# Retention V as tokens by features, in one doubled chunk, in a one-layer hybrid decoder kernel

## What is computed

```python
h = rmsnorm(x, g_mix)
q_sb, k_sb, v_sb, q_r, k_r, v_r, g_r, gate_sb, gate_ret = split_cols(h @ w_in)
...
q_r = rotary(to_heads(q_r, RET_HEADS))
k_r = rotary(to_heads(k_r, RET_HEADS)) * (RET_QK_DIM ** -0.5)
y_r = retention_chunkwise(q_r, k_r, to_heads(v_r, RET_HEADS))
y_r = from_heads(head_rmsnorm(y_r, ret_norm_gain)) * jax.nn.silu(g_r)
```

## Time and profile before

| what | value |
|---|---|
| median of 3 runs | 907.36 us (907.21 to 907.68) |
| the profiled execution | 907.26 us, its span on the core 905.5 us |
| TensorE busy | 895.5 us, 99% of the span |
| VectorE, ScalarE busy | 515.8 us (57%), 399.7 us (44%) |
| share of TensorE in the chain that ended last | 91% |
| the four pairs | to about 308 us of the span |

### The profile page before, as it was taken

One profiled execution on the slowest core, in us unless ns is written; L12 is line 12 of the kernel. 1 busy time (PEld: TensorE's weight loads), 2 busy tenths in 40 slices (PEclk: granted clock), 3 DMA queues, 4 the chain that ended last, 5 costly groups with the idle time before them and its releaser, 6 DMA issues.

```text
span 905.5 us, 11499 instructions
## 1 busy us (share of the span) xinstructions
PE 895.5 (99%) x4092; PEld 726.9 (80%) x4092; DVE 515.8 (57%) x653; ACT 399.7 (44%) x519; POOL 18.0 (2%) x19
## 2 busy tenths in 40 slices
PE   9999999999999999999999999999999999999998
PEld 7777777777787888888787888888888888888786
DVE  7797677677676443333455556655566543333354
ACT  6656746746746532232345433333333332323431
POOL 1410000000000000000000000000000000000000
PEclk9999999999999999999999999999999999999999
DMA  7114114114114153223322322222222332322131
GB/s 287 70 45 166 48 40 168 46 38 166 52 35 152 48 207 105 83 91 104 117 93 93 116 93 93 93 103 104 94 93 93 90 101 88 105 87 93 61 140 73
DMA packets 28553, 89.93 MB, mean 99 GB/s; under 512 B 3920, under 2 KB 4960, under 8 KB 28400
## 3 DMA queue, kind: packets, MB, share of 16 engines
q1 hardware_dynamic: 27232, 85.87, 27.4%
q10 hardware_dynamic: 1072, 3.67, 1.3%
q0 software_dynamic: 224, 0.06, 0.1%
HBM read 84.34 MB, written 2.10 MB: 95 GB/s over the span
## 4 chain that ended last, share of the span: by engine, by line
PE 91%; DVE 6%; ACT 2%; issue 1%; DMA 1%; SPq 0%; ACTq 0%; DVEq 0%
PE dense L360 28%; PE dense L361 28%; PE dense L362 28%; PE z L417 2%; DVE fs L1102 1%; DVE lo L1105 1%; DVE w_lo L1102 1%; PE aty L448 1%; DMA fs<-in_xT 1%; DVE fs L1286 1%; PE aty L362 1%; PE aty L361 1%; PE aty L360 1%; PE aty L406 1%; ACT w_hi L677 1%
## 5 line engine op out<-in xcount | busy, mean ns | idle before, releaser
L360 PE MATMUL dense<-hi,w_hi 128*128 128x512 f32 x1168 | 462.9, 396 | 1.5 <-DVE lo L1105 0.9
L362 PE MATMUL dense<-hi,w_lo 128*128 128x512 f32 x1168 | 455.2, 390 | 0.0
L361 PE MATMUL dense<-lo,w_hi 128*128 128x512 f32 x1168 | 454.9, 390 | 0.0
L1102 DVE TENSOR_TENSOR w_lo<-w_f,w_hi 128x1024 fp32r<-128x1024 f32 (+2 forms) x160 | 185.6, 1160 | 226.1 <-ACT w_hi L677 225.5
L360 PEld LDWEIGHTS dense<-hi,w_hi 128*128 128x128 f32 x1168 | 219.3, 188 | 52.3 <-issue 4.5
L362 PEld LDWEIGHTS dense<-hi,w_lo 128*128 128x128 f32 x1168 | 219.2, 188 | 46.5
L361 PEld LDWEIGHTS dense<-lo,w_hi 128*128 128x128 f32 x1168 | 219.5, 188 | 43.2 <-issue 1.0
L677 ACT CAST w_hi<-w_f 128x1024 fp32r<-128x1024 f32 (+2 forms) x160 | 158.3, 990 | 181.6 <-PE dense L362 179.0
L662 ACT ACTIVATE fs<-fs 128x512 f32<-128x512 f32 (+2 forms) x79 | 55.4, 707 | 80.7 <-DVE fs L1102 41.5
L1102 DVE TENSOR_TENSOR fs<-fs 128x512 f32<-128x512 f32 (+2 forms) x119 | 87.7, 743 | 3.7 <-ACT fs L709 0.5
L1102 DVE TENSOR_TENSOR lo<-fs,hi 128x512 f32 (+3 forms) x65 | 49.2, 764 | 40.9 <-ACT hi L1037 20.1
(11 more groups left out here) (98 smaller groups left out, 436.6 us busy)
## 6 DMA issues: line engine op xcount, KB each, us to landing
w_f<-in_w_in SPq DMA_DIRECT2D x52, 512.0 KB, 3.3
w_f<-in_w_up SPq DMA_DIRECT2D x44, 512.0 KB, 3.1
w_f<-in_w_down SPq DMA_DIRECT2D x16, 512.0 KB, 3.5
w_f<-in_w_b SPq DMA_DIRECT2D x8, 512.0 KB, 3.2
w_f<-in_w_out SPq DMA_DIRECT2D x8, 512.0 KB, 3.1
w_f<-in_w_pg SPq DMA_DIRECT2D x8, 512.0 KB, 3.1
w_f<-in_w_down SPq DMA_DIRECT2D x8, 384.0 KB, 3.0
fs<-in_xT SPq DMA_DIRECT2D x4, 512.0 KB, 7.0
```

What stands on the lines that cost most here:

```text
L360: mm(out, w1, x1, start=start, stop=False, skip_group_check=skip)
L361: mm(out, w1, x0, start=False, stop=False, skip_group_check=skip)
L362: return mm(out, w0, x1, start=False, stop=stop, skip_group_check=skip)
L1102: return nc.vector.tensor_tensor(out, a, b, op).then_inc(done, 1)
```

## The change

The two V chunks of a pair become one double chunk, `r_v`. The stationary side is now `h` (128 features by 128 tokens, four token blocks) and the moving side is one `k` block of both chunks' weights, 2 x 128 = 256 columns out of two ring slots. The result stands as tokens by features at once, token blocks 0 and 1 in bank 1, 2 and 3 in bank 2. So `turn_v` of chunks 7 and 8 and their copies out of the banks go, and the splits (`high_rv`, `low_rv`) read the two banks directly, at the start of the next `front`; chunk 1 and chunk 2 of that front wait for them (`free_bank`). `r_v` begins once the weights of both chunks are there, and `s_used` rises by 2 at its end. Its 16 steps (one `k` block for half of the tokens each) take the hooks of chunks 7 and 8, of which the head 1 values stand one step later in pairs 1 to 3. `ahead(j, 8)` moves on both engines from the end of `back` to between the two splits in `front`. In the first pair V now uses the normalised `h`, not the raw input, so `low_h(7)` moves forward. Key blocks 2 and 3 of the retention scores become one group: both stand side by side in `z` (384 columns), are masked by one instruction of 512 elements, split together, and their value products stand together at (2, 1). `y_raw` moves in front of `norm_qk(j, 1)` on ScalarE.

```diff
-RAW_OF = {0: 0, 1: 1, 2: 2, 3: 3, 4: 4, 7: 5, 8: 6}
-RAW_X = 8
+RAW_OF = {0: 0, 1: 1, 2: 2, 3: 3, 4: 4}
+RAW_X = 7
+EVACS = 7
...
-        w_hi = [sb(f"w_hi{r}", [P, 8, P], F32R) for r in range(RING)]
+        hi_ring = sb("w_hi", [P, RING, 8, P], F32R)
+        w_hi = [hi_ring[:, r, :, :] for r in range(RING)]
...
+            def r_v(j, hooks, before):
+                c = SLOTS * j + 7
+                pe.wait_ge(s_wlo, c + 2)
+                for step in range(2 * KD):
+                    k, half = step // 2, step % 2
+                    if before and half == 0:
+                        pe.wait_ge(*before[k])
+                    for i in (2 * half, 2 * half + 1):
+                        rows = slice(i * P, (i + 1) * P)
+                        out = bank[1 + half][:, (i % 2) * 2 * P:(i % 2 + 1) * 2 * P]
+                        w1, w0 = hi_ring[:, 1:3, k, :], lo_ring[:, 1:3, k, :]
+                        ins = split3(out, hi[:, T_H + k, rows], lo[:, T_H + k, rows], w1, w0, start=(k == 0 and i % 2 == 0),
+                                     stop=(k == KD - 1), skip=True)
+                    if step == 2 * KD - 1:
+                        ins.then_inc(s_used, 2)
+                    if step in hooks:
+                        hooks[step]()
...
             def free_bank(j, s):
-                pe.wait_ge(s_evac, SLOTS * j + s - 2)
+                if s in (1, 2):
+                    pe.wait_ge(s_raw_done, RAWS * j + s - 2)
+                else:
+                    pe.wait_ge(s_evac, EVACS * j + max(s - 2, 0))
...
-                places = {(0, 1): at(r_scores, prev, 0), (0, 3): at(turn_v, prev, 8, (s_raw_done, RAWS * j - 1)),
-                          (0, 6): at(r_scores, prev, 1), (1, 0): at(r_values, prev, 0), (1, 3): at(r_scores, prev, 2),
-                          (1, 6): at(r_values, prev, 1), (2, 0): at(r_scores, prev, 3), (2, 2): at(r_values, prev, 2),
-                          (2, 5): at(r_values, prev, 3)}
+                places = {(0, 1): at(r_scores, prev, 0), (0, 6): at(r_scores, prev, 1), (1, 0): at(r_values, prev, 0),
+                          (1, 3): at(r_scores, prev, 2), (1, 6): at(r_values, prev, 1), (2, 1): at(r_values, prev, 2)}
...
-                    later = 0
+                    later = 1
...
-                places[8, 6] = at(turn_v, j, 7, (s_atlo, 3 * j + 3))
-                for s in range(3, SLOTS):
+                for s in range(3, RAW_X):
...
+                free_bank(j, 8)
+                before = {k: (s_h, 1 + max(H_ORDER.index(x) for x in range(k + 1))) for k in range(KD)}
+                r_v(j, {KD * (s - 7) + k: places[s, k] for s in (7, 8) for k in range(KD) if (s, k) in places},
+                    before if prev is None else None)
... ScalarE, front
-                evac(prev, 8)
+                high_rv(prev, 0)
+                ahead(prev, 8)
+                high_rv(prev, 1)
                 y_move(prev, 1)
                 r_high(prev, 0)
                 ahead(j, 0)
-                high_v(prev, 2)
...
-                r_high(prev, 3)
...
+                y_raw(prev)
                 norm_qk(j, 1, 3 * j + 1)
-                y_raw(prev)
... VectorE, first_back
+                low_h(7)
                 low_rot(0, 0)
                 ahead(0, 7)
-                low_h(7)
-                evac_x(7)
... VectorE, front
             def front(j, prev):
+                low_rv(prev, 0)
+                ahead(prev, 8)
+                low_rv(prev, 1)
                 r_masked(prev, 0)
                 r_low(prev, 0)
                 ahead(j, 0)
-                low_v(prev, 2)
...
-                r_masked(prev, 3)
-                r_low(prev, 3)
... VectorE, back, its end
                 low_y(prev)
-                ahead(j, 8)
-                low_v(j, 1)
```

More of the change, by code:

```diff
@@ L213, in at_row, with r_group, r_width, r_pair @@
             return flat(t)[:, first * P:first * P + width(kb)]
-        def r_pair(t, i):
-            at = T_AT + 2 * (i % 2)
-            return t[:, at:at + 2, 0:width(i)]
+        def r_group(g):
+            return ((0,), (1,), (2, 3))[g]
+        def r_width(g):
+            return (SEQ, 3 * P, 3 * P)[g]
+        def r_pair(t, g):
+            at = T_AT + 2 * (g % 2)
+            return t[:, at:at + 2, 0:r_width(g)]
+        def r_diagonals(g):
+            blocks = z[:, :, 0:r_width(g)].rearrange("p h (b c) -> p h b c", c=P)
+            return blocks[:, :, 0:2 * len(r_group(g)) - 1:2, :]
+        def rv_rows(t, half):
+            return t[:, T_RV:T_RV + 2, 2 * half * P:(2 * half + 2) * P].rearrange("p h (b d) -> p h b d", b=2)
+        def rv_bank(half):
+            return bank[1 + half][:, :].rearrange("p (b h d) -> p h b d", b=2, h=2)
         def sb_v(hd):
@@ L477, in r_scores, with r_values @@
                 else:
[L478 to L483, removed]
+                    pe.wait_ge(s_ralo, 3 * j + g)
+                at = 0
+                for i in r_group(g):
+                    ins = heads_scores(i, T_RK, T_RQ, slice(i * P, SEQ), at)
+                    at += width(i)
+                ins.then_inc(s_zr, 1)
+            def r_values(j, g):
+                if g == 0:
                     pe.wait_ge(s_ysraw, 2 * j + 2)
@@ L486, in r_values @@
                     pe.wait_ge(s_raw_done, RAWS * j + 7)
[L487 to L492, removed]
-                ins.then_inc(s_vr, 1)
+                pe.wait_ge(s_ralo, 3 * j + g + 1)
+                at = 0
+                for i in r_group(g):
+                    cols, row = slice(i * P, (i + 1) * P), slice(at, at + width(i))
+                    for hd in range(2):
+                        ins = split3(aty[:, 1 + hd, i * P:SEQ], hi[:, T_RV + hd, cols], lo[:, T_RV + hd, cols],
+                                     r_pair(hi, g)[:, hd, row], r_pair(lo, g)[:, hd, row], start=(i == 0),
+                                     stop=(i == NT - 1), skip=True)
+                    at += width(i)
+                ins.then_inc(s_vr, 1)
+            def r_v(j, hooks, before):
[15 more added lines that the diff above has]
+                        hooks[step]()
             def warm_up():
@@ L542, in back @@
                 places[8, later + 3] = at(sb_values, j, 1, 0)
-                places[8, 6] = at(turn_v, j, 7, (s_atlo, 3 * j + 3))
-                for s in range(3, SLOTS):
-                    if prev is not None or s in (5, 8):
+                for s in range(3, RAW_X):
+                    if prev is not None or s == 5:
                         free_bank(j, s)
                     hooks = {k: places[s, k] for k in range(KD) if (s, k) in places}
-                    raw = prev is None and s < RAW_X
-                    before = {k: (s_h, 1 + max(H_ORDER.index(x) for x in range(k + 1)))
-                              for k in range(KD)} if prev is None and s == RAW_X else None
                     out = aty[:, s - 2, :] if prev is None and s in (3, 4) else None
-                    chunk(SLOTS * j + s, s % RING, s % 3, KD, T_X0 if raw else T_H, hooks, before=before, out=out)
+                    chunk(SLOTS * j + s, s % RING, s % 3, KD, T_X0 if prev is None else T_H, hooks, out=out)
+                free_bank(j, 8)
+                before = {k: (s_h, 1 + max(H_ORDER.index(x) for x in range(k + 1))) for k in range(KD)}
+                r_v(j, {KD * (s - 7) + k: places[s, k] for s in (7, 8) for k in range(KD) if (s, k) in places},
+                    before if prev is None else None)
             def stat_x():
@@ L739, in high_rot, with high_v, high_rv @@
                 nc.scalar.copy(hi[:, T_RQ + t, :], fs[:, A_RAW + (3 + t) % 2, :]).then_inc(s_rhi, 1)
[L741 to L748, removed]
+            def high_v(j):
+                act.wait_ge(s_vt, j + 1)
+                for hd in range(2):
+                    ins = nc.scalar.copy(sb_v(hd)[:, :, 0, :], v_turned(hd))
+                ins.then_inc(s_vhi, 1)
+            def high_rv(j, half):
+                act.wait_ge(s_used, SLOTS * j + 9)
+                nc.scalar.copy(rv_rows(hi, half), rv_bank(half)).then_inc(s_vhi, 1)
             def high_y(j):
@@ L1231, in low_rot, with low_v, low_rv, r_masked @@
                 tt(lo[:, T_RQ + t, :], fs[:, A_RAW + (3 + t) % 2, :], hi[:, T_RQ + t, :], ALU.subtract, s_raw_done)
[L1233 to L1252, removed]
+            def low_v(j):
+                dve.wait_ge(s_vhi, 3 * j + 1)
+                for hd in range(2):
+                    ins = nc.vector.tensor_tensor(sb_v(hd)[:, :, 1, :], v_turned(hd), sb_v(hd)[:, :, 0, :],
+                                                  ALU.subtract)
+                ins.then_inc(s_raw_done, 1)
+            def low_rv(j, half):
+                dve.wait_ge(s_vhi, 3 * j + 2 + half)
+                tt(rv_rows(lo, half), rv_bank(half), rv_rows(hi, half), ALU.subtract, s_raw_done)
+            def r_masked(j, g):
+                dve.wait_ge(s_zr, 3 * j + g + 1)
+                d, n = r_diagonals(g), len(r_group(g))
```

(10 more changed lines are left out.)

59 lines of the change are left out of this document (24 added, 35 removed).

## The result

The changed kernel takes 929.55 us (median; 929.43 to 930.73), the kernel before beside it 907.32 us: the ratio is 1.0247 (95% interval 1.0229 to 1.0265), 22 us slower. The profiled execution took 930.73 us, its span is 928.9 us; it is the slowest of the four, 1.2 us above the median. The forecast was 922.7 us in a range of 916 to 931.5.

The account below looks back on a forecast made before the run. TensorE, busy 99% of the span, was taken as the bound. Own work -3.2, hole +14.0, waits -1.8, +4.5 and +2.0 gave +15.5 us on 907.26, forecast 922.7 us, range 916 to 931.5.

Parts of the forecast that it names:

- the hole: TensorE stands still in front of `r_v` until chunk 8's weights are ready: +3.5 us per pair, +14.0 us in all.
- the clock falls: Rival: each hole in front of `r_v` brings TensorE to half rate, +8.8 us, 931.5 us; chance 0.09.
- the granted clock should stay at full: Sign for the changed kernel: no fall of the clock; a fall behind the hole would make the prediction wrong.
- the rival with 178 ns for each matmul: Rival: `r_v`'s matmuls take 178 ns each, +5.7 us per pair in place of +0.5, stated as 943.5 us; chance 0.04.
- `r_v` itself: 96 matmuls of 256 columns at 118 ns take 11.36 us against 10.88 for two V chunks: +0.5 us per pair.
- 256-column matmuls are slower in a long row: Rival: in `r_v`, stationary-block loading or the two-run moving side slows matmuls to 178 ns, stated as 943.5 us; chance 0.04.
- Transposes and grouped scores: TensorE's own work: two transpose hooks go, -0.9 us per pair; merging the narrow score block saves 0.4 us.
- Wait (a): First head 1 value product's wait for `y_out` goes in pairs 1 to 3; -0.5 in the first; -1.8 us together.
- Wait (b): `r_scores(1)` waits for `r_low(0)`, 0.7 us in pairs 1 to 3; 2.4 us in the first with `r_scores(0)`; +4.5 us.
- Wait (c): Transposes at (3, 3) wait for ScalarE's copy of chunk 2; merge's saving unearned in three pairs, 0.25 lost besides: +2.0 us.
- ready in time: Rival: chunk 8's weights end before chunk 7's place, no hole; 908.7 us, or 905 with smaller waits; chance 0.08.

Follow-up runs that it names:

- e2_hole_filled: Changed kernel with 14 matmuls of 512 columns, result unread, in front of the wait of `r_v`; 921.64 us, ratio 1.0153 to the kernel before.
- e1: Changed kernel with chunk 8's weights prepared one group of stick-breaking scores earlier on ScalarE and VectorE; 909.03 us, ratio 1.0017 to the kernel before.
- e3: Kernel before, without `r_v`, with one edit: chunk 7 also waits for the weights of chunk 8; 929.82 us, ratio 1.0247.
- e5: Kernel of e1 with ScalarE copying chunk 2 out in front of the two `y_square` steps, not behind; 906.07 us, ratio 0.9981 to the kernel before.
- e4: Kernel before with only key blocks 2 and 3 grouped (merged mask, split and value products, `y_raw` moved); 908.23 us, ratio 1.0005.

## Why the prediction was right, and where not

The direction held, and so did the main term, the hole; the time lay in the range. But the likeliest case was given as 922.7, and the measured time is 6.9 us above it. The step that failed is the choice between the forecast and the rival *the clock falls*, to which I gave 0.09: it came true in addition to all the rest. The prediction itself says that the granted clock should stay at full and that it is wrong if the clock falls behind the hole. By that sign it was wrong, and that the time lay in the range is due to the range reaching up to this rival's 931.5, 2 us above what was measured. The sum without the clock is what e2_hole_filled ran, 921.64 us.

Two sums of the prediction are slightly off: 907.26 + 15.5 is 922.8 and not 922.7, and the rival with 178 ns for each matmul comes to 922.7 + 4 x 5.7 = 945.5 and not 943.5. Neither changes the argument.

The starts of the 384-column retention score block, in all four pairs, divide the loss (us, from the timelines; the last row is the last matmul of the kernel):

| pair | before | after | behind by | grew since the row above | of it the clock | rest |
|---|---|---|---|---|---|---|
| first | 79.89 | 86.92 | 7.03 | 7.03 | 2.5 | 4.5 |
| second | 148.58 | 161.81 | 13.23 | 6.20 | 1.5 | 4.7 |
| third | 217.22 | 235.18 | 17.96 | 4.73 | 1.55 | 3.2 |
| fourth | 285.89 | 309.82 | 23.93 | 5.97 | 2.8 | 3.2 |
| end | 901.13 | 924.58 | 23.45 | -0.48 | 0 | -0.5 |

The clock's part is the length of `r_v` less that in e2_hole_filled. The table is of the profiled executions, so it ends at 23.45 and not at the 22.2 by which the medians differ. The rest sums to 15.1 us; the prediction's sum was 15.5.

- **The hole.** 3.5 us per pair was predicted, 3.47 to 3.52 measured. e1 takes it away and e3 makes it alone. Right.
- **`r_v` itself.** 118 ns for 256 columns was taken, 119 measured, so 96 cost 11.5 and not 11.4 us. Rival *256-column matmuls are slower in a long row* is dead, and the two-run moving side costs nothing that can be seen. The isolated-matmul formula of the Trainium skill ("TensorE: Matmul & The Clock Gate", "Back-to-back issue gap") gives 109 ns, an estimate from that page; no stretch of `r_v` shows that.
- **Transposes and grouped scores.** Between the matmul before the grouped hook and the second one behind it:

```profile
92.30 0.39 PE L386 MATMUL dense<-hi,w_lo 128*128 128x512 f32 x1
...
93.80 0.40 PE L385 MATMUL dense<-lo,w_hi 128*128 128x512 f32 x1
```

  That is 1.50 us, and without the chunk's own two distances 1.04. Alone the two blocks cost 0.75 (153.96 to 155.17 in the trace of before, less the same two distances) and 0.69 before, so 0.4 us are saved, as taken from the earlier trace rows.
- **Wait (a)** for `y_out` has no line any more in the list of waits. Right: in pairs 1 to 3 nothing is left of it, and in the first pair 0.24 us is (0.36 us between starts, 72.56 to 72.92, where 0.12 is the usual distance) of 0.74 before (66.02 to 66.99, where 0.23 is), so 0.5 was gained, as taken.
- **Wait (b), `r_scores(1)`.** Predicted 0.7 us in pairs 1 to 3; measured, from start to start less the 0.32 us that this place takes without a wait, 0.4 and 0.5 in the last two but 1.5 in the second, where `r_scores(0)` waits another 0.4. The rows of the second pair:

```profile
151.37 0.69 DVE L1149 TENSOR_TENSOR fs<-fs 128x512 f32<-128x512 f32 x1 [1.39 <-DMA fs<-fs]
...
155.77 0.50 PE L441 MATMUL z<-hi 64*128 64x512 f32 x2 [0.35 <-DVE lo L1149]
...
158.42 0.69 DVE L1149 TENSOR_TENSOR lo<-dense,hi 128x512 fp32r<-128x512 f32 x1
159.02 0.42 DVE L1149 TENSOR_TENSOR z<-z,cst 128x256 f32<-128x256 f32 x1
160.53 1.22 DVE L1149 TENSOR_TENSOR lo<-z,hi 128x1024 fp32r<-128x1024 f32 x1 [1.08 <-ACT hi L812]
...
161.81 0.44 PE L441 MATMUL z<-hi 64*128 64x384 f32 x2 [1.43 <-DVE lo L1149]
```

  VectorE's rotation at 151.37 is 1.4 us late, and the wait is for the swap DMA. That moved everything behind it: rotary k, then the V splits (158.42), the mask (159.02), the low part (to 161.75), and the score block at 161.81. I had costed the swap as shifted with the list; in the third pair it was, in the second not. From the issue of the swap to this rotation are 5.43 us here and 3.96 in the third pair. The traces of the other kernels say more: the second pair of each kernel with `r_v` has this wait, of 1.0 to 1.8 us, but for e2_hole_filled, where the same score block waits 0.38 us; no kernel without `r_v` has it there. So it comes with the change; why, and why not in e2_hole_filled, is not settled. In the first pair the two waits of `r_scores` cost 2.4 us in all, less 0.3 that stood there before. Together that is 4.9 us where 4.5 was predicted; that the sum came so near is partly luck, since the single terms are off both ways.
- **Wait (c), (3, 3).** ScalarE's copy and the transposes, in the `front` of the third pair:

```profile
183.07 0.58 ACT L760 COPY fs<-dense 128x512 f32<-128x512 f32 x1
...
183.77 0.44 PE L430 MATMUL aty<-cst,fs 128*128 128x128 f32 x2 [0.84 <-ACT fs L760]
```

  They answer to the earlier trace rows: from the matmul before, at 182.55, to the transposes 1.22 us, 1.0 us of wait where before it was 0.28. 0.7 more, three times, 2.1 us; predicted 2.0. e5 shows the cause, e4 that the grouping alone brings it.
- **The rival *ready in time*** said 908.7 us with waits (b) and (c) left. e1 is that rival made true on purpose: 909.03 us.
- **The clock.** The rule of the Trainium skill ("TensorE: Matmul & The Clock Gate", "Part 1: The HAM clock gate") that an idle array drops to half rate and must work to leave it, held here four times out of four, and four times in e3. I priced it right on average from the warm-up rows (2.2 us per hole; 2.1 measured, from 1.5 to 2.8) and weighed it wrong: "the hole is short" was no evidence, since the trace before had no hole after the start, and a rule without a row against it should have had more than 0.09.

## What to carry to other kernels

When a step is made to need two inputs at once, look up when the second is ready in the old trace, before anything else: here one row (weights ready at 130.68, the place at 127.24) held nearly two thirds of the loss, and moving one entry in each of two lists took 20.5 of 22 us back. A hole of 3.5 us in a busy TensorE is to be charged with a fall of the clock as well, here 2.1 us each; behind the waits of up to 1.5 us in e1_weights_ready it stayed full, and nothing between the two was tried. If such a hole can't be avoided, matmuls that nobody reads can pay for themselves, here 7.9 us. And a saving on TensorE shows only where TensorE sets the time: the grouped scores earned nothing until ScalarE's list gave way.

## What the runs showed of the hardware

- With a hole of 3.5 us the granted clock fell each time, eight holes in two kernels, the changed one and e3_old_with_wait; in the changed kernel in the hole or up to 1.1 us after work had begun again, and it was full again 4.3 to 6.2 us after that beginning. With the hole filled but for 0.3 us (14 matmuls of 0.227 us in 3.48, an estimate) it stayed, four times.
- At 1.2 GHz 256 columns took 0.213 us, at 2.4 GHz 0.119: the time lost is a little less than half of the stretch.
- The fall of the clock is not the same in every run of one kernel: the mean granted clock of the four executions of the changed kernel was 0.988, 0.990, 0.991 and 0.991, and their times 930.73, 929.63, 929.43 and 929.47 us.
